# Second FFN of a hybrid decoder step: down units one by one among the gate units, low parts of the hidden products in two places

## The reference

```python
def _swiglu(x, w_gate, w_up, w_down):
    return (jax.nn.silu(x @ w_gate) * (x @ w_up)) @ w_down
...
    h = h + 0.5 * _swiglu(_rms(h, p['g_ffn2']), p['w_ffn2_gate'], p['w_ffn2_up'], p['w_ffn2_down'])
```

## Time and profile before

| | us |
|---|---|
| median of 3 runs (1331.95 to 1334.77) | 1333.83 |
| the profiled execution | 1333.54 |
| its span | 1331.7 |
| PE busy | 1285.5 (97%) |
| DVE busy | 786.8 (59%) |
| ACT busy | 516.0 (39%) |
| POOL busy | 368.2 (28%) |

### The profile page before, as it was taken

How to read it: one execution, slowest core, us unless ns; L and a number is a source line. 1 busy time by engine, 2 the same in 40 slices (tenths; PEclk the granted TensorE clock), 3 DMA queues, 4 the chain that set the end, 5 groups by cost and what they waited for, 6 DMA issues and landing times.

```text
span 1331.7 us, 28531 instructions
## 1 busy us (share of the span) xinstructions
PE 1285.5 (97%) x11292; PEld 1184.4 (89%) x11292; DVE 786.8 (59%) x1398; ACT 516.0 (39%) x950; POOL 368.2 (28%) x393
## 2 busy tenths in 40 slices
PE   7999999999999999999999998999979999999997
PEld 7999999999999998966777665899979999999997
DVE  6335325333436797634444464554897988977964
ACT  5232221222225212233323344345555465466454
POOL 0218327125523001352222220032222222222202
PEclk9999999999999999999999999999989999999999
DMA  6223222322313321369999999444456686686721
GB/s 246 87 72 110 80 71 68 100 73 77 104 56 127 128 85 45 116 236 316 331 344 337 338 327 340 174 150 122 104 126 144 163 203 142 161 210 139 174 79 68
DMA packets 101993, 212.23 MB, mean 159 GB/s; under 512 B 12785, under 2 KB 26514, under 8 KB 101554
## 3 DMA queue, kind: packets, MB, share of 16 engines
q1 hardware_dynamic: 87586, 184.51, 42.6%
q0 software_dynamic: 11264, 19.41, 8.4%
q10 hardware_dynamic: 3024, 6.69, 1.3%
HBM read 200.87 MB, written 9.69 MB: 158 GB/s over the span
## 4 chain that ended last, share of the span: by engine, by line
PE 77%; DVE 10%; issue 4%; ACT 3%; DMA 3%; POOL 3%; SPq 1%; ACTq 0%; DVEq 0%; POOLq 0%
PE d L2169 37%; PE e L2276 9%; PE d L2276 8%; PE e L2514 7%; DMA kv<-kv_src 2%; PE e L2546 2%; PE e L2565 2%; DVE w_lo L1417 2%; PE d L2578 1%; PE d L2599 1%; PE e L2549 1%; PE d L2189 1%; DVE h_lo L1566 1%; SPq L546 1%; DVE ws_lo L1528 1%
## 5 line engine op out<-in xcount | busy, mean ns | idle before, releaser
L1417 DVE TENSOR_TENSOR w_lo<-raw,w_hi 128x1024 fp32r<-128x1024 f32 (+2 forms) x127 | 151.8, 1195 | 196.9 <-ACT w_hi L772 196.0
L772 ACT CAST w_hi<-raw 128x1024 fp32r<-128x1024 f32 (+2 forms) x127 | 123.6, 973 | 294.3 <-PE d L2169 276.9
L2169 PE MATMUL d<-x_hi,w_hi 128*128 128x272 f32 x976 | 205.0, 291 | 8.7 <-DVE w_lo L1770 6.8
L2169 PE MATMUL d<-x_hi,w_lo 128*128 128x272 f32 x976 | 202.7, 289 | 0.0
L2169 PE MATMUL d<-x_lo,w_hi 128*128 128x272 f32 x976 | 202.1, 289 | 0.0
L1528 DVE TENSOR_TENSOR ws_lo<-wr,ws_hi 128x512 fp32r<-128x512 f32 (+1 forms) x224 | 151.5, 683 | 41.7 <-ACT ws_hi L888 40.8
L2169 PEld LDWEIGHTS d<-x_hi,w_hi 128*128 128x128 f32 x976 | 154.3, 189 | 11.5 <-DVE w_lo L1770 6.8
L888 ACT CAST ws_hi<-wr 128x512 fp32r<-128x512 f32 (+1 forms) x224 | 128.7, 581 | 89.3 <-PE e L2276 42.9
L2169 PEld LDWEIGHTS d<-x_lo,w_hi 128*128 128x128 f32 x976 | 154.3, 190 | 0.0
L2169 PEld LDWEIGHTS d<-x_hi,w_lo 128*128 128x128 f32 x976 | 153.2, 190 | 0.0
L1392 POOL DMA_INDIRECT kr<-kr_src,gidx x64 | 61.2, 957 | 171.6 <-PE e L2549 160.7
(11 more groups left out here) (437 smaller groups left out, 3137.4 us busy)
## 6 DMA issues: line engine op xcount, KB each, us to landing
kv<-kv_src SPq DMA_DIRECT2D x256, 256.0 KB
wr<-w_gu SPq DMA_DIRECT2D x100, 256.0 KB, 3.9
raw<-w_gu SPq DMA_DIRECT2D x47, 512.0 KB, 3.6
raw<-w_post SPq DMA_DIRECT2D x34, 512.0 KB, 4.3
wr<-w_gu POOLq DMA_DIRECT2D x40, 256.0 KB, 5.3
wr<-w_d2b SPq DMA_DIRECT2D x40, 192.0 KB, 2.9
raw<-w_d1b SPq DMA_DIRECT2D x16, 384.0 KB, 3.2
raw<-w_in SPq DMA_DIRECT2D x10, 512.0 KB, 3.6
```

Source lines behind the costliest of these rows:

```text
L772: nc.scalar.copy(w_hi[:, s % 2, 0:n, :], raw[:, raw_pos(s), 0:n, :]).then_inc(S.hi_done, 1)
L1417: nc.vector.tensor_tensor(w_lo[:, s % 2, 0:n, :], raw[:, raw_pos(s), 0:n, :], w_hi[:, s % 2, 0:n, :].bitcast(FP), ALU.subtract).then_inc(S ...
L2169: ins = mm(out[:, b, :], w[:, pos, c0 + k, :], x[:, k, b * HALF:(b + 1) * HALF], start=first, stop=stop)
```

## The change

Three things. First, `UNITS2` is written anew. Before, the list had the two first gate units of the next block and then all four down units of a block; now they alternate. With g for gate and d for down units, around the first block:

- before: g6 g7 d0.0 d0.1 d0.2 d0.3 g8 g9 g10 g11 g12 g13
- now: g6 g7 d0.0 g8 d0.1 g9 d0.2 d0.3 g10 g11 g12 g13

The second block goes the same way, and around the last: before g18 g19 d2.0 d2.1 d2.2 d2.3 g20 g21, now g18 g19 g20 d2.0 d2.1 d2.2 d2.3 g21. Second, the low parts of a pair are made in two places (`LO_A_AT`, `LO_B_AT`), the second three products behind the first in most pairs; pair 0 is treated a unit later than before (its steps move from products 5, 7, 8 to 12, 14, 15 and 18), and pairs 4 and 7 too. Third, DVE makes the hidden products of chunks 0 and 1 itself (`multiplied`), POOL those of 2 to 20, at places that `hidden_at` gives: those of 8 and 9 come together with 10 behind the last down unit of the first block, those of 14 and 15 with 16.

```diff
+    UNITS2 = [("g", j) for j in range(HEAD, BLOCKS[0])]
+    for b, nb in enumerate(BLOCKS[:-1]):
+        ahead = [("g", j) for j in range(sum(BLOCKS[:b + 1]), sum(BLOCKS[:b + 2]))]
+        down = [("d", (b, i)) for i in range(KC // 2)]
+        if b + 2 < NB:
+            UNITS2 += ahead[0:2] + down[0:1] + ahead[2:3] + down[1:2] + ahead[3:4] + down[2:] + ahead[4:]
+        else:
+            UNITS2 += ahead[0:3] + down + ahead[3:]
...
-        n = UNIT_OF["g", 2 * q + 1] if 2 * q + 1 >= HEAD else -1
+        n = UNIT_OF["g", 2 * q + 1] if 2 * q + 1 >= HEAD else 0
         b = next(b for b in range(NB) if q < sum(BLOCKS[:b + 1]) // 2)
         if b and q == sum(BLOCKS[:b]) // 2:
             free = AT["P4", UNIT_OF["d", (b - 1, KC // 2 - 1)]]
-            return AT["P1", n + 2], free, free + 1
-        return AT["P1", n + 2], AT["P3", n + 1], AT["P6", n + 2]
+            return AT["P1", n + 2], free, free + 1, free + 1
+        if b and q == sum(BLOCKS[:b]) // 2 + 1:
+            n = UNIT_OF["d", (b - 1, KC // 2 - 1)] + 1
+            return AT["P4", n], AT["P5", n + 1], AT["P7", n + 2], AT["P6", n + 2]
+        return AT["P1", n + 2], AT["P3", n + 1], AT["P6", n + 2], AT["P5", n + 2]
+
+    def hidden_at(j):
+
+        n = UNIT_OF["g", j]
+        b = next(b for b in range(NB) if j < sum(BLOCKS[:b + 1]))
+        if b and j >= sum(BLOCKS[:b]) + 2:
+            n = max(n, UNIT_OF["d", (b - 1, KC // 2 - 1)] + 1)
+        return min(n + 1, NU - 1)
...
-                if n >= 1 and not dense(n - 1):
-                    hidden(pair_of(n - 1))
+                for j in range(HEAD, sum(BLOCKS) - 1):
+                    if hidden_at(j) == n:
+                        hidden(j)
...
+                if k in (0, 6):
+                    multiplied(k // 6)
                 if k in SUMS_AT:
                     hidden_sums(SUMS_AT[k])
-                if k in LO_AT:
-                    hidden_lo(LO_AT[k])
+                if k in LO_A_AT:
+                    hidden_lo(LO_A_AT[k], 0)
+                if k in LO_B_AT:
+                    hidden_lo(LO_B_AT[k], 1)
```

More of the change, by code:

```diff
@@ L299, in build @@
     E_LAST = T_FFN2 + 2 * HEAD
-    UNITS2 = []
-    for b, nb in enumerate(BLOCKS):
-        j0 = sum(BLOCKS[:b])
-        UNITS2 += [("g", j) for j in range(j0, j0 + nb) if j >= HEAD and not (b and j < j0 + 2)]
-        if b + 1 < NB:
-            UNITS2 += [("g", j) for j in range(j0 + nb, j0 + nb + 2)]
-            UNITS2 += [("d", (b, i)) for i in range(KC // 2)]
+    UNITS2 = [("g", j) for j in range(HEAD, BLOCKS[0])]
[6 more added lines that the diff above has]
+            UNITS2 += ahead[0:3] + down + ahead[3:]
     NU = len(UNITS2)
@@ L1282, in ffn2 @@
                 add_block(n, x)
-            for j in range(HEAD):
-                hidden(j)
             for n in range(-1, NU):
```

29 lines of the change are left out of this document (15 added, 14 removed).

## The result

The changed kernel takes 1369.74 us (median of 4 runs, 1365.36 to 1371.41) beside 1334.3 us (1331.95 to 1338.06) for the kernel before on the same chip: 1.026 times as long, with a 95% interval of 1.0239 to 1.0282. The profiled execution took 1371.41 us, span 1369.6. Forecast were 1353.7 us and a range from 1339 to 1362: slower, as said, but by 35 us and not by 20.

A forecast was written before the change was run, and what follows sets the result against it. PE is busy for 1285.5 of 1331.7 us, so only its waits can be gained and longer waits are paid in full. The terms sum to +20.2 on 1333.5, giving 1353.7 us, range 1339 to 1362.

The forecast's parts named there:

- Term 1: Start of the second FFN: two products leave POOL and pair 0's sums and splits leave the stretch, -8.1 us.
- Term 2: Pair 0 to pair 1: late hand-over of hv delays POOL and its adding transfers, losses at products 22 and 25, +7.2 us.
- Term 3: Ahead of the first down unit: h_lo's second half comes later, +2.7 us in the first block, +5.2 in the second.
- Term 4: Behind the last down unit: hv is held until product 88, so product 92 starts late; twice +2.3 us.
- Term 5: Last block, pair 8: as in the second block, losses at products 179 and 181, +2.4 us.
- 6, two upb waits: Pairs 4 and 7: two waits of 1.3 us for upb go, as the splits stand away from the differences, -3.1 us.
- 7, end: The end: product 221 loses 1.8 us, and chunk 20's late multiplication on POOL costs PE 5.8; +4.8 us net.
- Term 8: Clock: three new idle times of over 2.3 us at 1.5 us each, +4.5 us, bounds 0 to 9.
- the rule that had been weighed: Of a two-SBUF-input DVE operation and a GpSimd one, the first to start keeps the shared port; would give 1355.6 us.
- the faster rival: POOL's hidden(2) and its like: hv is free early enough that three products hide the hand-over; 1329.6 us, chance 0.09.
- longer clock losses: Bracket shared with no gain at the start: the time lies from 1358 to 1366 us, chance 0.12.
- Half covered: Delays hold, but transfers land early or waits fall together, halving four losses: +9.2 us, 1342.7 us, chance 0.15.

## Why the forecast was right in direction and wrong in size

Each stretch, split into what the clock took (slow matmuls at 0.1 us) and the rest, stands against its term:

| term | forecast | measured without clock |
|---|---|---|
| 1, start (clock included) | -8.1 | -7.9 |
| 2, pair 0 to pair 1 | +7.2 | +7.35 |
| 3, first down unit, block 0 | +2.7 | +2.7 |
| 3, block 1 | +5.2 | +6.9 |
| 4, behind the last down unit | +4.6 | +9.8 |
| 5, last block, pair 8 | +2.4 | +2.3 |
| 6, two upb waits | -3.1 | -3.1 |
| 7, end | +4.8 | +4.8 |
| 8, clock | +4.5 | +13.0 |
| interleaving itself | 0 | -0.7 |

Sum +20.2 against +35.2. Of the 15.0 us between them 8.5 lie in Term 8, 5.2 in Term 4 and 1.7 in Term 3's second block; the rest is -0.4.

**Term 1** held in its parts, though not as closely as -7.9 looks: against the other profiles of the same starts the gain is 5.7 to 8.8 us. The forecast had 3.1 us for POOL's quiet and 4.95 for pair 0's steps leaving the stretch. Product 8, up to which only the first can act, starts 3.1 us earlier (2.4 to 3.1 against all four old starts), and so it does with the multiplications alone, pair 0's steps being at their old places; the x sum takes 1.28 us in place of 3.21. The waits at products 11 and 13 are gone, as said. By the rule that had been weighed (the Trainium skill, SBUF — State Buffer, section "SBUF: two separate sides"), this operation, begun first, would have owed nothing to POOL; the traces do not agree: begun 0.4 us ahead of POOL, as far as POOL's start in a profile can be relied on, it was 1.9 us longer than without POOL's multiplication. The term itself does not decide between -8.1 and -6.2, as both lie within 5.7 to 8.8. What the multiplications alone left undone was the other part: with pair 0's steps at their old places, the wait at product 11 is longer and takes part of the gain back.

**Terms 2, 3 (first block), 5, 6 and 7** held within 0.2 us; with Terms 2 and 5 some of that is luck. In Term 2 the losses at products 22 and 25 were 1.7 and 6.7 us (idle time and 0.24), not 1.1 and 6.2, and the wait of 1.3 us at 27, which it had kept, was gone. In Term 5 the loss of 1.25 us at 181 did not come, and one of 1.2 at 174 did. A bound was added up wrong: in Term 3, 0.35 + 0.60 + 1.29 - 0.9 is 1.3, not 1.6, which would move the faster rival by 0.5 us. Term 3 in the second block had left out a wait of 0.96 us at product 104: DVE's low part of weights takes 1.81 us beside a multiplication of POOL that began 0.09 us earlier, as the rows above show. That these two hinder each other was argued from the start's rows and not tried apart here.

**The step whose mechanism failed is Term 4**, "ACT splits until T87 + 2.5, DVE from 3.7 to 5.9, POOL multiplies chunk 8 until 7.6". ACT and DVE did so (with T87 near 1109.2, the low parts ended 6.1 later), but POOL was not free: ahead of chunk 8 in its row stands an adding transfer whose plain load had not landed. The forecast had weighed such a thing at pair 0 and at pair 4, where a transfer stands behind a multiplication, and not the other way round. With the multiplication put first, the idle time was 1.98 us where the term had 2.05. So the hand-over was costed rightly and the queue in front of it was missed: 5 us without the clock, in two places, each of which came out above the term's upper bound of 3 (5.2 and 4.6).

**Term 8 failed in size, and weighs most.** It counted three new idle times at 1.5 us. Seven places took the clock down: at 25, 40 and 110 for 5.8 us together, at 92 and 162 for 4.4, at 179 for 1.5 and some 1.3 at the end. Two rules of the term were wrong. The price of 1.5 came from one wait of 2.31 us, while the waits of over 4 us in the changed kernel had 20 to 24 slow matmuls behind them, 2 us and more each. And an idle time near 2 us was taken as free, where it is so in 12 of 28 cases only. With a right Term 4 the forecast would still have been 10 us low.

Of the rivals, none came true; the time lay above all of their brackets, and of these "longer clock losses" (1358 to 1366, with 0.12) was nearest in number and in kind. "Half covered" rested on waits that fall together; they stood in places of their own, and the stretches add up. That the direction was forecast with 0.85 was well founded: of what was moved only the start, 7.9 us, and two small waits, 3.1, could gain, against three hand-overs. The signs that it had named for being right came too: product 13 starts 24.8 us behind product 0 and not 31.2 (3.8 us earlier by the profile's own time, as product 0 came 2.6 later), 20 us later, not 15, a wait of 6.42 us for ACT begins, with ACT waiting for a transfer, h_lo is waited for 3.57 and 4.83 us at two down units, and 1.66 and 5.50 us stand at the end.

**What stays open:** why an idle time of 1.8 to 2.3 us lowers the clock in some executions and not in others, and why 3.4 us can cost more than 5.5. Whether a fourth place for sl would make the interleaving free was not tried.
